# A kernel of two transformer blocks: the sums of its RMS norms as rows over all partitions, the first two tiles behind a norm taken together

## The reference

```python
def rms_norm(x, gain=None):
    y = xf * lax.rsqrt(jnp.mean(xf * xf, axis=-1, keepdims=True) + RMS_EPS)
...
for l in range(DEPTH):
    h = rms_norm(x) * (1.0 + scale_a) + shift_a
    x = x + gate_a * hybrid_mixer(h, cos, sin, w_in[l], ...)
    h = rms_norm(x) * (1.0 + scale_f) + shift_f
    x = x + gate_f * (jnp.square(jax.nn.relu(h @ w_mlp_up[l])) @ w_mlp_down[l])
```

## Time and profile before

| | |
|---|---|
| median of 3 runs | 4535.36 us (4529.16 to 4537.4) |
| profiled execution | 4530.36 us, its span 4528.6 us |
| PE busy | 4155.0 us, 92% |
| DVE busy | 2209.1 us, 49% |
| ACT busy | 1436.1 us, 32% |
| POOL busy | 174.8 us, 4% |
| granted TensorE clock | 0.966 of full speed, mean |

### The profile page before, as it was taken

One profiled execution on the slowest core, in us unless ns is written; L12 is line 12 of the kernel. 1 busy time (PEld: TensorE's weight loads), 2 busy tenths in 40 slices (PEclk: granted clock), 3 DMA queues, 4 the chain that ended last, 5 costly groups with the idle time before them and its releaser, 6 DMA issues.

```text
span 4528.6 us, 47207 instructions
## 1 busy us (share of the span) xinstructions
PE 4155.0 (92%) x18908; PEld 3143.7 (69%) x18908; DVE 2209.1 (49%) x3315; ACT 1436.1 (32%) x2332; POOL 174.8 (4%) x181
## 2 busy tenths in 40 slices
PE   6888889899999978889989999969999999999995
PEld 3566555588888866655668888856777777887774
DVE  6677455543443345545553333343364553546745
ACT  3323434321121233335431211213343343324422
POOL 2200000000000000000010000010000000000001
PEclk9999999899999999999989999989999999999997
DMA  5432200033332120110022222111111111115531
GB/s 202 161 112 84 91 14 1 28 102 93 95 101 66 47 70 24 61 45 1 16 64 75 71 72 63 47 65 47 43 43 47 43 43 56 52 61 214 174 133 47
DMA packets 93667, 325.13 MB, mean 72 GB/s; under 512 B 10376, under 2 KB 11176, under 8 KB 92362
## 3 DMA queue, kind: packets, MB, share of 16 engines
q1 hardware_dynamic: 74874, 250.28, 16.8%
q0 software_dynamic: 18576, 71.84, 5.1%
HBM read 287.47 MB, written 34.60 MB: 71 GB/s over the span
## 4 chain that ended last, share of the span: by engine, by line
PE 82%; DVE 11%; ACT 4%; issue 2%; DMA 0%; POOL 0%; SPq 0%; DVEq 0%; ACTq 0%
PE PS L958 55%; PE PS L1817 4%; PE PS L741 2%; PE PS L2837 2%; PE PS L2623 1%; PE PS L1291 1%; PE PS L1689 1%; PE PS L1544 1%; PE PS L2250 1%; PE PS L1538 1%; PE PS L1688 1%; PE PS L2277 1%; PE PS L2263 1%; PE PS L1718 1%; PE PS L664 1%
## 5 line engine op out<-in xcount | busy, mean ns | idle before, releaser
L958 PE MATMUL PS<-hi,WH 128*128 128x512 f32 x2816 | 1160.4, 412 | 114.9 <-issue 37.7
L958 PE MATMUL PS<-hi,WL 128*128 128x512 f32 x2816 | 1121.5, 398 | 0.0
L958 PE MATMUL PS<-lo,WH 128*128 128x512 f32 x2816 | 1115.0, 396 | 0.0
L958 PEld LDWEIGHTS PS<-hi,WH 128*128 128x128 f32 x2816 | 538.4, 191 | 280.6 <-issue 107.7
L958 PEld LDWEIGHTS PS<-hi,WL 128*128 128x128 f32 x2816 | 537.5, 191 | 120.4
L958 PEld LDWEIGHTS PS<-lo,WH 128*128 128x128 f32 x2816 | 538.8, 191 | 115.0 <-issue 5.7
L498 ACT ACTIVATE WH<-raw 128x1024 fp32r<-128x1024 f32 x304 | 319.9, 1052 | 735.7 <-PE PS L958 587.4
L508 DVE TENSOR_TENSOR WL<-raw,WH 128x1024 fp32r<-128x1024 f32 x264 | 322.7, 1222 | 205.5 <-ACT WH L498 205.3
L958 PE MATMUL PS<-ah,WL 128*128 128x512 f32 x1024 | 402.4, 393 | 0.0
L958 PE MATMUL PS<-ah,WH 128*128 128x512 f32 x1024 | 400.4, 391 | 0.0
L958 PE MATMUL PS<-al,WH 128*128 128x512 f32 x1024 | 399.4, 390 | 0.0
(11 more groups left out here) (425 smaller groups left out, 5427.8 us busy)
## 6 DMA issues: line engine op xcount, KB each, us to landing
adab<-in_w_ada POOLq DMA_DIRECT2D x120, 512.0 KB, 4.6
raw<-in_win SPq DMA_DIRECT2D x104, 512.0 KB, 3.6
raw<-in_up SPq DMA_DIRECT2D x64, 512.0 KB, 3.6
raw<-in_down SPq DMA_DIRECT2D x64, 512.0 KB, 3.6
raw<-in_dft SPq DMA_DIRECT2D x24, 512.0 KB, 4.3
sp_x<-X SPq DMA_DIRECT2D x24, 512.0 KB, 6.4
X<-sp_x SPq DMA_DIRECT2D x24, 512.0 KB, 5.4
raw<-in_wout SPq DMA_DIRECT2D x24, 512.0 KB, 3.6
```

Source lines behind the costliest of these rows:

```text
L958: mm = pe.matmul(bank[b + hf], w[:, k, :], r[:, k, HALF[hf]], start=k == 0 and w is wh and r is hi, stop=k == 7 and w is wl)
```

## The change

The eight column matmuls, the tiny 1/sqrt, the diagonal, the spreading matmuls and the copy are gone from the four norms of the first block. Instead a matmul of ones (128x128) by the row of partial sums (128x512) gives each half's sums on all partitions at once, in banks 4 and 5; the squares' last term is added by a second matmul of the pair instead of by DVE. ACT makes Ln, Exp and a Square of each half, DVE a Newton step (three operations) of 128x512, and the first zq, hi and lo go by halves. POOL has no part any more: DVE makes all zq and lo, ACT one hi for each i, in the second block too. For norm (0, 0) ACT's wait for the stored filter spectra stands ahead of its first Ln now.

T1 gets banks 2 and 3 behind all three kinds of norm, and its first k's stand between those of T0: T0 k0, k1, T1 k0, T0 k2, T1 k1, T0 k3, k4, T1 k2, T0 k5, T1 k3, T0 k6, T1 k4, T0 k7, T1 k5, k6, k7. The model times move: a layer is 1238.5 long instead of 1308, the first tile stands 8.5 behind a norm instead of 30.

```diff
-    return 190.0 + 1308.0 * l
+    return 190.0 + 1238.5 * l
 
 
 
@@ -132,9 +132,20 @@
 
 MIXED_TILE = 17.2
 
+
+FIRST = 8.5
+
+def first_tile(at):
+
+    return lambda k: at + 2.4 * k
+
+def second_tile(at):
+
+    return lambda k: at + 1.45 + (2.4 * (1, 2, 4, 5, 6)[k] if k < 5 else 16.8 + 1.4 * (k - 5))
+
 def win_at(l, i):
 
-    return layer_at(l) + 30 + TILE * min(i, 3) + MIXED_TILE * max(i - 3, 0)
+    return layer_at(l) + FIRST + TILE * min(i, 3) + MIXED_TILE * max(i - 3, 0)
...
-    return layer_at(l) + (548 if part else 0)
+    return wout_at(l, 1, 8) + 1.5 if part else layer_at(l)
 
 def mlp_at(l, q):
-    return layer_at(l) + 578 + TILE * q
+    return norm_at(l, 1) + FIRST + TILE * q
+
+def mlp_end(l, q):
+    return mlp_at(l, 0) + 18.4 if q == 0 else mlp_at(l, q + 1)
...
+        def sums_of(l, part, hf):
 
             if part:
-                return [(WO_DVE, ("squares", l, 7, hf)) for hf in range(2)]
+                return [(m.osa[:, HALF[hf]], WO_DVE["squares", l, 6, hf]), (m.osq[:, hf, :], WO_ACT["square", l, 7, hf])]
             if l:
-                return [(UP_DVE, ("squares", 0, 7, hf)) for hf in range(2)]
-            return [(SS_DVE, (7, hf)) for hf in range(2)]
-
-        def sums_of(l, part):
-            return m.osa if part else halves_of_rl if l else m.ssa
+                return [(m.rl[:, hf, :], UP_DVE["squares", 0, 6, hf]), (LAST_SQUARE[hf], UP_ACT["square", 0, 7, hf])]
+            return [(m.ssa[:, HALF[hf]], SS_DVE[7, hf])]
...
+            parts = [sums_of(l, part, hf) for hf in range(2)]
+            n = len(parts[0])
+            for i in range(n):
+                for hf in range(2):
+                    yield norm_at(l, part) + (-0.9 if i == n - 1 else -4) + 0.7 * hf
+                    if i == hf == 0:
+                        free_norm_banks(pe, l, part)
+                    rows, ready = parts[hf][i]
+                    pe.wait_ge(*ready)
+                    mm = pe.matmul(bank[4 + hf], ones[:, :], rows, start=i == 0, stop=i == n - 1)
+                    if i == n - 1:
+                        mm.then_inc(*NO_PE.next("sums", l, part, hf))
...
+            for hf in range(2):
+                yield at + 2 + 2.6 * hf
+                y, t = rs[:, HALF[hf]], zq[:, 3, HALF[hf]]
+                dve.wait_ge(*NO_ACT["again", l, part, hf])
+                dve.scalar_tensor_tensor(out=t, in0=bank[4 + hf], scalar=EPS * S, in1=t, op0=ALU.add,
+                                         op1=ALU.mult).then_inc(*DVE_OWN.next())
+                dve.wait_ge(*DVE_OWN.now())
+                dve.tensor_scalar(t, t, -0.5 / S, 1.5, ALU.mult, ALU.add).then_inc(*DVE_OWN.next())
+                dve.wait_ge(*DVE_OWN.now())
+                dve.tensor_tensor(y, y, t, ALU.mult).then_inc(*NO_DVE.next("rs", l, part, hf))
+                if hf:
+                    NO_DVE.at["rs", l, part] = NO_DVE.n
+                else:
+                    dve.wait_ge(*ADA_OK[l, 40 if part else 16])
+                dve.wait_ge(*NO_DVE["rs", l, part, hf])
+                dve.scalar_tensor_tensor(out=zq[:, 0, HALF[hf]], in0=X[:, 0, HALF[hf]], scalar=sc[:, 0:1], in1=y, op0=ALU.mult,
+                                         op1=ALU.mult).then_inc(*NO_DVE.next("scaled", l, part, 0, hf))
+            for hf in range(2):
+                yield at + 5.3 + 1.9 * hf
+                dve.wait_ge(*NO_ACT["high", l, part, 0, hf])
+                dve.scalar_tensor_tensor(out=lo[:, 0, HALF[hf]], in0=zq[:, 0, HALF[hf]], scalar=sh[:, 0:1],
+                                         in1=hi[:, 0, HALF[hf]].bitcast(F), op0=ALU.add, op1=ALU.subtract).then_inc(
+                    *NO_DVE.next("low", l, part, 0, hf))
+            NO_DVE.at["low", l, part, 0] = NO_DVE.n
+            for i in range(1, 8):
+                yield at + 4.5 + 2 * i
                 z = zq[:, i % 4, :]
+                if i > 3:
+                    dve.wait_ge(*NO_DVE["low", l, part, i - 4])
+                dve.scalar_tensor_tensor(out=z, in0=X[:, i, :], scalar=sc[:, i:i + 1], in1=rs[:, :], op0=ALU.mult,
+                                         op1=ALU.mult).then_inc(*NO_DVE.next("scaled", l, part, i))
+                yield at + 6.6 + 2 * i
                 dve.wait_ge(*NO_ACT["high", l, part, i])
+                dve.scalar_tensor_tensor(out=lo[:, i, :], in0=z, scalar=sh[:, i:i + 1], in1=hi[:, i, :].bitcast(F),
+                                         op0=ALU.add, op1=ALU.subtract).then_inc(*NO_DVE.next("low", l, part, i))
...
         def norm_act(act, l, part):
             at = norm_at(l, part)
             hi, lo, zq, rs = m.norm2 if part else m.norm1
             sc = mod1[:, 8 * part:8 * part + 8]
             sh = MODS[l][:, 24 * part:24 * part + 8]
+            yield at - 1.5
+            act.preload_act_table_set(EXPLN)
             if l == 0 and part == 0:
                 for o in range(2):
                     act.wait_ge(*FS_OUT[o][1, 3])
+            for hf in range(2):
+                yield at + 0.1 + 1.9 * hf
+                y = rs[:, HALF[hf]]
+                act.wait_ge(*NO_PE["sums", l, part, hf])
+                act.activation(y, bank[4 + hf], ACT.Ln, bias=t_eps, scale=1.0 / S).then_inc(*ACT_OWN.next())
+                act.wait_ge(*ACT_OWN.now())
+                act.activation(y, y, ACT.Exp, bias=0.0, scale=-0.5).then_inc(*ACT_OWN.next())
+                act.wait_ge(*ACT_OWN.now())
+                act.activation(zq[:, 3, HALF[hf]], y, ACT.Square, bias=0.0).then_inc(*NO_ACT.next("again", l, part, hf))
+            for hf in range(2):
+                yield at + 4.6 + 1.9 * hf
+                act.wait_ge(*NO_DVE["scaled", l, part, 0, hf])
+                act.activation(hi[:, 0, HALF[hf]], zq[:, 0, HALF[hf]], ACT.Identity, bias=sh[:, 0:1]).then_inc(
+                    *NO_ACT.next("high", l, part, 0, hf))
+            for i in range(1, 8):
+                yield at + 5 + 2 * i
+                act.wait_ge(*NO_DVE["scaled", l, part, i])
+                act.activation(hi[:, i, :], zq[:, i % 4, :], ACT.Identity, bias=sh[:, i:i + 1]).then_inc(
+                    *NO_ACT.next("high", l, part, i))
...
+        def norm_low(l, part, k, hf):
+
+            return NO_DVE["low", l, part, 0, hf] if k == 0 and l < 2 else NO_DVE["low", l, part, k]
...
+            at = first_tile(win_at(l, 0)) if i == 0 else second_tile(win_at(l, 0)) if i == 1 else win_at(l, i)
+            yield from gemm_pe(pe, TILE_OF["win", l, n][0], at, hi, lo, win_bank(i), first if i < 2 else None, free,
+                               1.4 if i < 3 else 2.0)
...
-                        act.activation(m.sq1[:, :] if n else m.rl[:, hf, :], X[:, n, HALF[hf]], ACT.Square,
-                                       bias=0.0).then_inc(*UP_ACT.next("square", l, n, hf))
+                        act.activation(LAST_SQUARE[hf] if n == 7 else m.sq1[:, :] if n else m.rl[:, hf, :], X[:, n, HALF[hf]],
+                                       ACT.Square, bias=0.0).then_inc(*UP_ACT.next("square", l, n, hf))
...
             d = layer_norm_parts(0)[1]
             for i in range(8):
                 yield SECOND + 28 + 2 * i
+                if i == 0:
+                    dve.wait_ge(*LS_ACT["rs", 0])
+                    dve.wait_ge(*ADA_OK[2, 24])
+                dve.scalar_tensor_tensor(out=d[i], in0=d[i], scalar=mod1[:, i:i + 1], in1=m.lrs[:, :], op0=ALU.mult,
+                                         op1=ALU.mult).then_inc(*NO_DVE.next("scaled", 2, i))
                 yield SECOND + 31 + 2 * i
                 dve.wait_ge(*NO_ACT["high", 2, i])
...
+                act.wait_ge(*NO_DVE["scaled", 2, i])
+                act.activation(m.hi3[:, i, :], d[i], ACT.Identity, bias=m2[:, i:i + 1]).then_inc(*NO_ACT.next("high", 2, i))
...
+        def project_tiles_pe(pe, tiles):
+            for p in tiles:
+                def first(k, hf):
                     pe.wait_ge(*NO_DVE["low", 2, k])
 
                 def free(hf):
+                    if p > 1:
+                        pe.wait_ge(*PJ_ACT[p - 1 if p > 2 else 0, hf])
+                    else:
+                        pe.wait_ge(*UP_DVE["x", 1, 3, 6 + p])
+                at = project_at(0) + 0.3
+                at = first_tile(at) if p == 0 else second_tile(at) if p == 1 else project_at(p) + 0.3
+                yield from gemm_pe(pe, TILE_OF["win2", PROJECTED[p]][0], at, m.hi3, m.lo3, project_bank(p),
+                                   first if p < 2 else None, free, 1.45)
 
         def project_act(act):
```

More of the change, by code:

```diff
@@ L907, in norm_pool @@
-        def norm_pool(pool, l, part):
-            zq, rs = (m.norm2 if part else m.norm1)[2:]
-            for i in BY_POOL:
-                yield norm_at(l, part) + 8.1 + 2 * i - 1
-                pool.wait_ge(*NO_ACT["rs", l, part])
-                if i > 3:
-                    pool.wait_ge(*NO_DVE["low", l, part, i - 4])
-                pool.tensor_tensor(zq[:, i % 4, :], X[:, i, :], rs[:, :], ALU.mult).then_inc(
-                    *NO_POOL.next("scaled", l, part, i))
```

(43 more changed lines are left out.)

162 lines of the change are left out of this document (42 added, 120 removed).

## The result

The changed kernel takes 4586.1 us (4574.9 to 4589.3, four runs) against 4536.4 for the kernel before (4529.2 to 4551.3): ratio 1.0101, interval 1.007 to 1.0132. The forecast was 4562, with a range of 4540 to 4592.

The account below looks back on a forecast made before the run. PE bounds the kernel (82% of the span's chain), so changes count where PE waits. Loads 53.2 plus second block 9.1, less norm gains 35.2, give +27.1 us on the 4535.4 median: 4562, range 4540 to 4592.

Parts of the forecast that it names:

- The table loads decide: Layer 0's mixer: 87 function-table loads on ACT instead of 12, three terms together +53.2 us, the deciding term.
- The attention's 25: MLA with attention, layer 0: 14 units, 28 loads, 1.8 us a unit; 25 us lost, between 12.6 and 35.9.
- MLA's 13.3: Layer 0's MLA ahead of attention: 24 loads make PE 13.3 us later, between 0 and 30.8.
- 0.85: Gated outputs, first pair: 0.85 us added for PE's slow clock behind longer waits.
- the Ln's load hides in idle time like the 1.70: MLA with attention: the load ahead of each unit's Ln lies in ACT's idle time; the Exp's can't.
- Gated outputs, 14.9: Gated attention's outputs, eight units: ACT is the path, nothing hides the loads; 9.8 plus 5.1, 14.9 us lost.
- Norms: First block's four norms: second tile ends earlier, gains of 6.5, 8.8, 9.8 and 10.1 us, together 35.2.
- the second block's loss: Second block's norm: T1's first k waits for its WL and holds up T0's other k's; 9.1 us lost.
- Hidden loads: Rival: fewer than 26 of the loads' 96 us reach PE, so the kernel is faster; 4519 with 10 exposed; chance 0.08.
- rough cancelling: Rival: 17 to 35 us of loads exposed, time within 9 us of before, 4535; chance 0.12.
- All loads exposed: Rival: every load moves a queue that PE waits on, +70 us, 4605; chance 0.10.
- drain: Rival: the engine also drains as long as it loads, doubling each exposed load, +53 us, 4615; chance 0.04.

Follow-up runs that it names:

- e1: Changed kernel with layer 0's hand-made table load put behind the rope's last Sin (15 loads instead of 87): 4515.3 us.
- e2: Kernel before with only layer 0's hand-made table load moved ahead of the third Sin (86 loads instead of 12): 4611.8 us.
- e6a: e1 with one hand-made table load ahead of each Ln of MLA's unit norms in layer 0, 26 loads more: 4527.3 us.
- e6c: e1 with loads both ahead of each Ln and between Ln and Exp in MLA's layer 0 unit norms, 52 more: 4564.9 us.
- e3: Changed kernel with the second block's T1 weight operations WH and WL put among the norm's rows, behind the fourth lo: 4565.1 us.
- e4: Changed kernel with T1 wholly behind T0, as before, but still in banks 2 and 3: 4607.2 us.
- e5: Changed kernel with DVE's order in all five norms as zq of i + 1, then lo of i: 4557.0 us.
- e6b: e1 with one hand-made table load between each Ln and Exp of MLA's unit norms in layer 0, 26 more: 4532.4 us.
- e7b: e7, but with the table load where the changed kernel has it and the rope's angles made earlier: 4469.9 us.
- e7: Changed kernel with the repairs of e1, e3 and e5 together: 4470.7 us.

## Why the prediction was right, and where its sizes were off

- *The table loads decide.* Right, and shown from both sides (e1, e2). Without them the change is a gain of half a percent.
- *The attention's 25.* The term that was mis-sized: 34.4. So was MLA's 13.3, with 17.4. What it left out is the clock: the units were followed as waits, and only the gated outputs have a term for it (0.85). The windows show 24.1 and 10.0 us more idle time of PE, close to or below the 25 and 13.3, and 10.3 and 7.8 more of busy time for the same matmuls. This splits what was measured; how long PE would have waited at the high level no run shows. A second step was too kind, "the Ln's load hides in idle time like the 1.70": true of that row, but in e6a 14 such loads, 18.0 us long, cost 10.6 in the attention. The changed kernel's ACT and PE (timeline) show how a load can miss the idle time:

```profile
736.31 0.60 ACT L1792 ACTIVATE pT<-PS 128x512 f32<-128x512 f32 x1 [3.29 <-PE PS L1732]
736.93 1.28 ACT L1619 ACT_TABLE_LOAD   x1
738.23 0.69 ACT L1619 ACTIVATE adab<-PS,col 128x512 f32<-128x512 f32 x1
738.93 1.28 ACT L1622 ACT_TABLE_LOAD   x1
740.23 0.63 ACT L1622 ACTIVATE adab<-adab 128x512 f32<-128x512 f32 x1
740.76 0.58 ACT L1792 ACTIVATE pT<-PS 128x512 f32<-128x512 f32 x1
741.39 1.16 PE L1747 MATMUL PS<-pT,vt 128*128 128x128 f32 x8 [1.34 <-ACT pT L1792]
```

The 3.29 us of idle time end with a copy of the probabilities; the unit's four instructions stand behind it with no gap, and ahead of the second copy, for which PE waited 1.34 us. The two loads, 2.57 us, are more than that wait. The idle time was before the first copy, where it hides nothing. I had named the copies as late too, but priced them from five units followed. That the rest of e6c's excess, the 7.3 us of idle time, is slack which the first load uses up is argued, not shown.
- *Gated outputs, 14.9.* Measured 17.3: ACT was the path, as forecast; PE's wait for the ACT line grew from 13.5 to 27.0 (some 25 forecast).
- *Norms.* Gains of 7.7, 7.6, 10.0 and 9.5 for 6.5, 8.8, 9.8 and 10.1; the second block's loss 9.2 for 9.1. e3 and e4 confirm its cause. The row behind the 1.0 us of a sum matmul shows x4 where the prediction counts two matmuls; in the changed kernel the two matmuls of L848 leave a row of x4 as well, and take 1.88 us.
- *On the rivals.* Hidden loads and rough cancelling are excluded by the result and by e2. All loads exposed was nearer than I gave it: 69 of 96 us came through, and the median lies 24 above the likeliest value and 19 below that rival's 4605. No drain was seen: the load of 736.93 is followed by the Ln 0.02 behind its end. That a set holds both functions, as the Trainium skill says (ScalarE: Activation LUTs, Table sets: the hidden batching unit), e1 agrees with: one load by hand serves all of them; without one standing, each function brought its own.
- *The sum.* Had the loads' term been 69.1, the sum would be +43, and the forecast 4578. The measured medians differ by 49.7, with an interval of some 32 to 60. The time fell inside the range, 6 below its upper end, because the range was wide enough for the missing term, not because the term was in it. Two of its bounds were also worked out wrongly: half the Exp's loads in the attention are 9.0 us, not 12.6, and the two lower bounds take away 25.7, not some 20. Nothing of the result hangs on these.

## What to carry to other kernels

Where a program orders instructions by model times, a load of a function table is an instruction with a place like any other: after moving anything, count the loads. Idle time on an engine hides an added instruction only if it lies directly ahead of it and not ahead of something that it then delays; look at what stands behind. Price the waits also by what they do to PE's clock: here a third of what the loads cost in MLA and attention was the same matmuls taking longer. When two tiles are interleaved, everything that the second needs (its weights too) must stand ahead of its first use, or it holds up the first.

## What the runs showed of the hardware

In the filter stage PE runs at the low of its two levels at first: two matmuls 0.43 us apart, though the granted clock in that row reads 1.00. By the spacing of the matmuls it went to the high level at about 65 us in the profiled executions of before, e1, e3, e4, e5, e6b and e6c, at about 90 in those of the changed kernel, e2 and e7b, and at 70 to 77 in e6a and e7, with the same code and the same work ahead of it. This alone moves an execution by up to 13 us (last filter evacuation at 186.3 to 199.5), 0.3%. It may be a part of why runs of one kernel lie 10 us and more apart; only profiled executions show it. Nothing in the traces shows what decides it.

In the attention of layer 0 more waiting went with a lower clock: the same 803 matmuls took 186.5 us of PE's time at 0.98 (e1), 189.2 at 0.97 (before), 199.4 at 0.94 (changed) and 206.5 at 0.90 (e3, with the same instructions there as the changed kernel).
